# Eleven pieces of the gate's projection move from the first unit of pairs into the quads

## Chip, core and metric

One NeuronCore of a Trainium2 chip runs the whole program in one launch. The metric is the device time of an execution in microseconds; lower is better. Engines are called by short names: PE (TensorE, matmuls and transposes), DVE (VectorE), ACT (ScalarE), POOL (GpSimd) and SP (SyncE, which here issues all the DMAs).

## What is computed

Two layers of a hybrid encoder over 768 tokens (a sequence of 256 and one of 512), width 2048, in fp32:

```python
h = rms_norm(x, ln_g[l])
qa, ka, va, ga, qb, kb, vb, gb, qc, kc, vc, gc = split(h @ w_in[l])
ya = window_sink_attention(...)        # mixer A: +-128 tokens, a sink, relative bias
yb = global_axial_attention(...)       # mixer B: dense, rotary
yc = dilated_mixture_attention(...)    # mixer C: (window, dilation) (128,1), (512,4), (2048,16), merged
mix = concat([ya * silu(ga), yb * silu(gb), yc * silu(gc)])
x = x + mix @ w_out[l]
```

The 32 heads have 64 columns each; mixers A and B have 12 query heads, C has 8 for each of three dilations. The gate is the product of h with 2048 columns of w_in.

## The kernel before, in words

Each layer has three stages. First the projection of all columns but the gate's, in nine slabs of 512 columns. Last the output product. Between them lies the attention, and the gate's projection is dealt out in pieces over it; this stage is what the change touches.

**Precision.** Each fp32 operand of a large product is split in two parts, hi (a rounded copy, made by ACT) and lo (the rest, made by DVE); a product is three matmuls, hi·hi, hi·lo and lo·hi.

**Steps.** The attention is a list of 216 steps, written out in Python before the program is built. Steps 0 to 23 are the quads (kind Q: the dilated parts of mixer C, four heads at a time, one token tile per item). They come in four units of six: steps 0 to 5 and 12 to 17 are open (dilation 4), 6 to 11 and 18 to 23 are packed (dilation 16, four classes in one tile). Steps 24 to 47 are the first unit of pairs (mixer A, two heads of an item, one head per step), then come the other pairs of A, C and B up to step 215.

**Turns.** All engines walk through one loop over turns i (232 of them per layer, N_LOOP), in a fixed order of instructions. In turn i PE does the scores of step i, then the gate's pieces of this turn, then the product with v of an earlier pair (PAIR_LAG 5), the transpose of the probabilities of step i-3 (T_LAG) and, for quads and C, the product with v of step i-4 (V_LAG). DVE adds the bias and takes the minimum of the scores of step i (find_minima), ACT takes the exponential (exp_step), DVE takes its reciprocal and POOL normalises one turn later in the pairs (NORM_LAG). DVE or ACT takes the quads' results out of their bank in turn i+5 (take_part for open, take_packed for packed items), and SP stores them (store_part). There are two banks for scores, so the scores of step i wait for the minima of step i-2.

**The gate.** There are 16 gate tiles of 128 columns; each takes 16 chunks of k times two halves of the tokens, so 512 pieces in a layer. A piece is three matmuls of 128 x 384. 16 pieces are done ahead of the loop, 20 behind step 215, and the 476 between them are dealt over the steps by piece_schedule, in proportion to a cost per step. PIECES_BY[i] is how many pieces are done by the end of turn i. Much else is timed from it by turn_of_piece:

- SPLIT_TURN: when ACT (split_hi, w_hi) and DVE (split_lo, w_lo) split a chunk of 128 x 512 gate weights. In the quads DVE does this behind the minima of the turn, ACT behind the exponentials.
- GATE_LOADS_AT: behind which item SP issues the next 512 KB of gate weights (two chunks; w_raw has three slots).
- DRAIN_TURN, TANH_AT, SILU_TURN, PRODUCT_TURN: when DVE takes a finished gate tile half out of its bank, ACT makes the tanh, POOL the silu and the product with the attention's result.

**SP's order.** For each item `it` from 4 on, SP waits for the scores of item it-4, loads the queries of item it (quad_t in the quads, 256 KB), stores parts of quads that are due, then loads keys, values, the blocks of the packed units (the values, laid out by class), the bias and last the gate weights that stand at this item. The blocks of unit 3 (steps 18 to 23) are loaded in four parts, at items 20 to 23; the product of step 18, in turn 22, needs all of them.

```python
for it in range(Q_SLOTS, N_ITEMS + 1):
    load_item(l, it)
    for i in PARTS_AT.get(it, ()): store_part(l, i)
    ...
    for u, c in BLOCKS_AT.get(it, ()): load_blocks(l, u, c)
    for b, heads in BIASES_AT.get(it, ()): load_bias(l, b, heads)
    ...
    for m in GATE_LOADS_AT.get(it, ()): load_weights(l, CHUNKS_IN // PER_LOAD + m)
```

Of the kernel before, what the change touches and what calls it, by code (L numbers as in the profile page):

```python
# [310 lines left out]
def packed(unit):  # L311

    return unit["kind"] == "Q" and unit["g"] == 2
# [6 lines left out]
def attention_items():  # L320

    order = [x for u in range(len(ATT_UNITS)) for x in unit_items(u)]
    items, steps = [], []
    for u, hp, t in order:
        unit = ATT_UNITS[u]
        lo, hi = next(x for x in SEQ_TILES if x[0] <= t < x[1])
        a, b = max(lo, t - unit["reach"]), min(hi, t + unit["reach"] + 1)
        for r in (None,) if hp is None else (0, 1):  # L330
            first = min(max(t * P - C_REACH, lo * P), hi * P - C_KEYS) if unit["kind"] == "C" else a * P
            tiles = (1 if packed(unit) else 4) if r is None else C_KEYS // P if unit["kind"] == "C" else b - a
            steps.append(dict(item=len(items), u=u, unit=unit, kind=unit["kind"], hp=hp, t=t, r=r, a=a, first=first,
                              tiles=tiles, last=r != 0))
        items.append(dict(u=u, unit=unit, kind=unit["kind"], hp=hp, t=t, step=len(steps) - 1))
    return items, steps


ITEMS, STEPS = attention_items()
# [225 lines left out]

def piece_schedule():

    cost = [3 if packed(st["unit"]) else {"Q": 1}.get(st["kind"], 8) for st in STEPS]
    done, now, between = [], 0, PIECES - PIECES_FIRST - PIECES_LAST
    for i in range(N_LOOP):  # L570
        if i < N_STEPS:
            now += cost[i]
            done.append(PIECES_FIRST + between * now // sum(cost))
        else:
            done.append(min(PIECES, PIECES - PIECES_LAST + PIECES_LAST * (i - N_STEPS + 1) // V_LAG))
    assert done[-1] == PIECES
    return done


PIECES_BY = piece_schedule()  # L580


# [2102 lines left out]
```

How the kernel before makes its waits and increments, by code:

```python
        def prob_copied(eng, l, i):  # L926
            if features_first(STEPS[i]) or not on_act(i):
                eng.wait_ge(pt_dve, l * DVE_COPIES[-1] + DVE_COPIES[i])
            else:
                eng.wait_ge(pt_act, l * ACT_COPIES[-1] + ACT_COPIES[i])
# [1 line left out]
        def turn_evacuated(eng, i):  # L933
            l, s, t, b, _ = TURNS[i]
            if s == "norm":
                eng.wait_ge(norm_lo, NORM_AT[l, s, t, b] + 1)
            else:
                eng.wait_ge(turned_lo, HEAD_AT[l, s, t] + 1)
# [17 lines left out]
        def quad_taken(eng, l, quad):  # L957
            item = QUADS[quad]
            if packed(item["unit"]):
                eng.wait_ge(packed_taken, l * N_PACKED + item["packed_no"] + 1)
            else:
                eng.wait_ge(part_taken, l * (N_QUADS - N_PACKED) + item["open_no"] + 1)
# [1 line left out]
        def bias_in(eng, l, b):  # L965
            sets = [x for x in BIAS_SETS if BIAS_NO[x] % 2 == b % 2]
            each_layer = sum(4 if x[1] is None else 2 for x in sets)
            in_layer = sum(4 if x[1] is None else 2 for x in sets if BIAS_NO[x] <= b)
            eng.wait_ge(bias_loaded[b % 2], 16 * (l * each_layer + in_layer))
# [5 lines left out]
        def stat_free(eng, pair):  # L976
# [3 lines left out]
            l, at = divmod(pair - STAT_SLOTS, N_PAIRS)  # L980
            old = PAIRS[at]
            if old["kind"] == "C":
                eng.wait_ge(merge_chain, 5 * (l * MERGES + old["merge_no"] // TT) + 5)
            else:
                eng.wait_ge(normed, l * NORMED[-1] + NORMED[old["step"]])
```

## Time and profile before

| | |
|---|---|
| Median of three executions | 2765.29 us (2764.78 to 2768.25) |
| The profiled execution | 2772.11 us, span 2769.8 us |
| Granted PE clock over the span | 0.994 of full speed |
| Busy: PE matmuls / PE weight loads / DVE / ACT / POOL | 99% / 88% / 58% / 43% / 28% |
| DMA | 442.52 MB, 160 GB/s |
| Quads, layer 0 / layer 1 | 651.0 to 706.3 / 2021.8 to 2082.7 us |

The span runs from the first to the last instruction. A matmul's busy time overlaps its neighbours' (they are pipelined, and their ends are modelled), so what a series of matmuls costs is read from start to start, and not from their durations. The granted clock of a stretch is the mean over it; PE has two levels, 2.4 GHz (1.00) and 1.2 GHz (0.50).

### The profile page before, as it was taken

The numbers are of one execution on the slowest core, as the hardware profiler recorded it, in microseconds if no ns is written. First come the engines' busy times: TensorE is split into PE (matmuls) and PEld (weight loads), VectorE is DVE, ScalarE is ACT, GpSimd is POOL, SyncE is SP. The second block draws the span as 40 slices with busy tenths as digits, with TensorE's granted clock in tenths as the row PEclk, the third lists the DMA queues.
The fourth block names the chain that finished last, engine by engine and source line by source line (L and its number), as shares of the span: only waits on it lengthen the run. The fifth ranks groups of instructions, "written<-read, shape, count | busy, mean of one in ns | idle before, by whom it ended". The sixth has DMA issues, their size and how long they took to land. (4 is left out here: it accounts for less than half of the span.)

```text
span 2769.8 us, 43315 instructions
## 1 busy us (share of the span) xinstructions
PE 2732.1 (99%) x14505; PEld 2447.6 (88%) x14505; DVE 1609.7 (58%) x3865; ACT 1184.4 (43%) x2813; POOL 763.8 (28%) x882
## 2 busy tenths in 40 slices
PE   8999999999999999999999999999999999999999
PEld 7888899988999999988888888999889999999887
DVE  3345644434676677677743465444346767776776
ACT  4322222224565566544542222222246655665443
POOL 0333333320343344300003334333203433443000
PEclk9999999999999999999999999999999999999999
DMA  5356566668544542464524565656774445325535
GB/s 175 106 183 200 180 185 188 181 179 233 142 132 123 128 112 82 177 219 130 197 85 142 176 195 173 200 170 188 191 218 134 117 118 149 101 69 217 192 122 182
DMA packets 436214, 442.52 MB, mean 160 GB/s; under 512 B 97591, under 2 KB 327127, under 8 KB 435996
## 3 DMA queue, kind: packets, MB, share of 16 engines
q1 hardware_dynamic: 435996, 439.77, 53.3%
q8 instruction: 118, 1.93, 0.3%
q14 instruction: 100, 0.82, 0.1%
HBM read 313.91 MB, written 125.75 MB: 159 GB/s over the span
## 5 line engine op out<-in xcount | busy, mean ns | idle before, releaser
L1834 ACT CAST w_hi<-w_raw 128x512 fp32r<-128x512 f32 x640 | 397.0, 622 | 697.8 <-PE bank L1605 430.6
L1603 PE MATMUL bank<-w_hi,act_hi 128*128 128x512 f32 x1728 | 689.2, 399 | 0.0
L2120 DVE TENSOR_TENSOR w_lo<-w_raw,w_hi 128x512 fp32r<-128x512 f32 x640 | 460.1, 722 | 384.9 <-ACT w_hi L1834 383.3
L1605 PE MATMUL bank<-w_hi,act_lo 128*128 128x512 f32 x1728 | 679.0, 393 | 0.0
L1604 PE MATMUL bank<-w_lo,act_hi 128*128 128x512 f32 x1728 | 677.6, 392 | 0.0
L1605 PEld LDWEIGHTS bank<-w_hi,act_lo 128*128 128x128 f32 x1728 | 372.6, 216 | 54.1
L1603 PEld LDWEIGHTS bank<-w_hi,act_hi 128*128 128x128 f32 x1728 | 373.3, 216 | 50.1
L1604 PEld LDWEIGHTS bank<-w_lo,act_hi 128*128 128x128 f32 x1728 | 373.3, 216 | 48.7
L1659 PE MATMUL bank<-act_hi,w_hi 128*128 128x384 f32 x1024 | 349.2, 341 | 0.0
L1661 PE MATMUL bank<-act_hi,w_lo 128*128 128x384 f32 x1024 | 346.3, 338 | 0.0
L1660 PE MATMUL bank<-act_lo,w_hi 128*128 128x384 f32 x1024 | 345.7, 338 | 0.0
L2561 POOL TENSOR_SCALAR prob<-prob,denom 128x256 f32<-128x256 f32 (+2 forms) x288 | 165.6, 577 | 399.1 <-DVE denom L2275 398.8
L1636 PE MATMUL bank<-w_hi,a_part 128*128 128x512 f32 x672 | 263.0, 391 | 2.7 <-DVE x_cols L2416 2.0
L1637 PE MATMUL bank<-w_lo,a_part 128*128 128x512 f32 x672 | 261.6, 389 | 0.0
L1638 PE MATMUL bank<-w_hi,a_part 128*128 128x512 f32 x672 | 261.5, 389 | 0.0
L2266 DVE TENSOR_TENSOR pt_lo<-bank,pt_hi 128x256 fp32r<-128x256 f32 (+2 forms) x288 | 154.0, 535 | 184.8 <-ACT pt_hi L1934 182.3
L2552 POOL TENSOR_TENSOR y<-y,gains 128x256 f32<-128x256 f32 (+1 forms) x144 | 159.9, 1123 | 265.5 <-DVE y L2153 265.5
L2186 DVE TENSOR_TENSOR turned<-bank,turned 128x512 fp32r<-128x512 f32 (+2 forms) x120 | 64.8, 556 | 277.4 <-ACT turned L1901 277.4
L1901 ACT CAST turned<-bank 128x512 fp32r<-128x512 f32 (+2 forms) x120 | 55.2, 481 | 364.2 <-PE bank L1581 355.8
L1660 PEld LDWEIGHTS bank<-act_lo,w_hi 128*128 128x128 f32 x1024 | 194.1, 190 | 4.2
L1709 PE MATMUL bank<-ident,prob 128*128 128x128 f32 x1128 | 195.7, 274 | 1.5 <-POOL prob L2561 0.9
L1659 PEld LDWEIGHTS bank<-act_hi,w_hi 128*128 128x128 f32 x1024 | 193.5, 189 | 4.1
(136 smaller groups left out, 4406.5 us busy)
## 6 DMA issues: line engine op xcount, KB each, us to landing
w_raw<-w_in SPq DMA_DIRECT2D x144, 512.0 KB, 4.8
w_sums<-sum_out SPq DMA_DIRECT2D x32, 1280.0 KB, 6.7
w_raw<-w_sums SPq DMA_DIRECT2D x80, 512.0 KB, 4.0
sum_in<-w_out SPq DMA_DIRECT2D x64, 512.0 KB, 5.6
heads_t<-turned SPq DMA_DIRECT2D x240, 128.0 KB, 2.4
q_t<-heads_t SPq DMA_DIRECT2D x192, 128.0 KB, 2.1
k_t<-keys_t SPq DMA_DIRECT2D x48, 384.0 KB, 5.8
w_raw<-w_out SPq DMA_DIRECT2D x32, 512.0 KB, 3.7
```

The source lines that it names most:

```text
L1603: pe.matmul(acc[t][:], hi, w_hi[:, W_AT[n]:W_AT[n] + SLAB], start=(k == 0), stop=False)
L1604: pe.matmul(acc[t][:], hi, w_lo[:, W_AT[n]:W_AT[n] + SLAB], start=False, stop=False)
L1605: last = pe.matmul(acc[t][:], lo, w_hi[:, W_AT[n]:W_AT[n] + SLAB], start=False, stop=(k == KC - 1))
L1636: pe.matmul(bank[at][:], hi[:, tokens], w_hi[:, W_AT[n]:W_AT[n] + SLAB], start=(j == 0), stop=False)
L1637: pe.matmul(bank[at][:], hi[:, tokens], w_lo[:, W_AT[n]:W_AT[n] + SLAB], start=False, stop=False)
L1638: last = pe.matmul(bank[at][:], lo[:, tokens], w_hi[:, W_AT[n]:W_AT[n] + SLAB], start=False, stop=(j == KH - 1))
L1659: pe.matmul(out, hi, act_hi[:, k, tokens], start=(k == 0), stop=False)
L1660: pe.matmul(out, hi, act_lo[:, k, tokens], start=False, stop=False)
L1661: last = pe.matmul(out, lo, act_hi[:, k, tokens], start=False, stop=(k == KC - 1))
L1709: last = pe.transpose(pt_bank[n % PT_BANKS][:, j * P:(j + 1) * P], prob[:, n % P_SLOTS, j * P:(j + 1) * P], ident[:])
L1834: nc.scalar.copy(w_hi[:, W_AT[n]:W_AT[n] + SLAB], w_raw[:, load % W_RAW, j, :]).then_inc(w_hi_done, 1)
L2120: nc.vector.tensor_tensor(w_lo[:, W_AT[n]:W_AT[n] + SLAB], w_raw[:, load % W_RAW, j, :], w_hi[:, W_AT[n]:W_AT[n] + SLAB].bitcast(F32), ALU ...
```

## The change

```diff
 def piece_schedule():
 
-    cost = [3 if packed(st["unit"]) else {"Q": 1}.get(st["kind"], 8) for st in STEPS]
+    first_pairs = min(st["u"] for st in STEPS if st["kind"] != "Q")
+    cost = [4 if packed(st["unit"]) else 3 if st["kind"] == "Q" else 6 if st["u"] == first_pairs else 8 for st in STEPS]
     done, now, between = [], 0, PIECES - PIECES_FIRST - PIECES_LAST
     for i in range(N_LOOP):
         if i < N_STEPS:
```

The cost of a packed quad's step goes from 3 to 4, that of an open quad's from 1 to 3, that of a step of the first unit of pairs from 8 to 6; all others stay at 8. Since the pieces are dealt in proportion, PIECES_BY changes, and with it the tables that are timed from it:

| | before | after |
|---|---|---|
| pieces in the quads' turns 0 to 23 | 14 | 25 |
| pieces in turns 24 to 47 | 58 | 44 |
| pieces in turns 48 to 215 | 404 | 407 |
| turns with one piece among 0 to 23 | 3, 6 to 11, 14, 17, 19 to 23 | 1 to 7, 9 to 20, 22, 23 (two in 8 and 21) |
| splits of gate chunks 4 to 11 in turns | 9, 15, 22, 25, 33, 35, 37, 38 | 5, 9, 12, 16, 30, 33, 35, 37 |
| third and fourth gate load in the loop, at item | 20, 29 | 14, 21 |
| tile 0's second half taken out, tile 1's first, in turns | 25, 32 | 16, 28 |

From gate tile 2 on the tables differ by at most two turns.

## Rows read from the trace of the kernel before

**Rows 1.** The page, busy time and share of each engine.

```profile
PE 2732.1 (99%) x14505; PEld 2447.6 (88%) x14505; DVE 1609.7 (58%) x3865; ACT 1184.4 (43%) x2813; POOL 763.8 (28%) x882
```

**Rows 2.** Busy time by stretch: us, PE, PEld, DVE, ACT, POOL, clock, DMA share, GB/s.

```profile
651.00:706.30 55.30, 48.03 (x358) 45.58 (x356) 35.26 (x166) 26.74 (x85) 1.99 (x2) 0.91 0.86 246
706.30:757.00 50.70, 50.70 (x332) 49.92 (x331) 32.71 (x141) 31.84 (x95) 20.17 (x31) 1.00 0.45 125
2021.80:2082.70 60.90, 52.98 (x357) 50.25 (x356) 34.86 (x166) 26.79 (x85) 2.01 (x2) 0.85 0.81 223
2082.70:2135.00 52.30, 52.30 (x336) 51.41 (x335) 33.07 (x142) 32.27 (x96) 20.55 (x31) 0.97 0.45 122
```

**Rows 3.** PE's timeline in the quads: start, us, instruction, idle before and its releaser.

```profile
659.52 0.33 PE L1689 MATMUL bank<-k_t,quad_t 128*128 128x128 f32 x1 [1.23 <-DMA quad_t<-heads_t]
...
678.46 0.30 PE L1689 MATMUL bank<-k_t,quad_t 128*128 128x128 f32 x1 [1.46 <-DVE part_out L2237]
...
702.76 1.21 PE L1731 MATMUL bank<-blocks,prob_t 128*128 128x260 f32 x2 [4.35 <-DMA blocks<-v_rows]
...
2032.63 0.63 PE L1684 MATMUL bank<-k_t,quad_t 128*128 128x64 f32 x4 [1.38 <-DMA quad_t<-heads_t]
...
2053.88 0.30 PE L1689 MATMUL bank<-k_t,quad_t 128*128 128x128 f32 x1 [1.26 <-DVE part_out L2237]
...
2079.14 1.21 PE L1731 MATMUL bank<-blocks,prob_t 128*128 128x260 f32 x2 [4.97 <-DMA blocks<-v_rows]
```

**Rows 4.** Busy time by finer stretches of the quads, columns as in rows 2.

```profile
659.52:673.93 14.41, 14.41 (x113) 13.83 (x114) 10.58 (x37) 5.03 (x16) 0.00 (x0) 1.00 0.86 238
673.93:683.68 9.75, 8.29 (x51) 7.54 (x51) 4.34 (x33) 6.10 (x23) 0.00 (x0) 0.82 1.07 301
683.68:702.76 19.08, 14.73 (x123) 14.28 (x122) 11.78 (x49) 7.79 (x23) 0.00 (x0) 0.92 0.93 269
702.76:706.29 3.53, 3.52 (x12) 3.14 (x13) 2.48 (x8) 1.35 (x4) 0.00 (x0) 0.50 0.18 58
...
2030.50:2049.56 19.06, 17.68 (x101) 16.91 (x100) 10.22 (x33) 4.80 (x15) 0.00 (x0) 0.73 0.76 198
2049.56:2059.10 9.54, 8.28 (x51) 7.53 (x51) 4.14 (x33) 6.10 (x23) 0.00 (x0) 0.82 0.92 243
```

**Rows 5.** PE's timeline: two gate pieces' starts, and scores in the first pairs.

```profile
643.24 0.34 PE L1659 MATMUL bank<-act_hi,w_hi 128*128 128x384 f32 x1
...
643.76 0.34 PE L1659 MATMUL bank<-act_hi,w_hi 128*128 128x384 f32 x1
...
722.21 0.42 PE L1695 MATMUL bank<-k_t,q_t 128*128 128x384 f32 x1
```

**Rows 6.** Timelines of DVE and ACT in layer 0's quads.

```profile
677.20 0.29 DVE L2237 CUSTOM_DVE_ANT_0 prob<-bank,bias 128x128 f32<-128x128 f32 x1 [2.14 <-DMA bias<-bias_rows]
...
684.14 1.28 ACT L1916 ACTIVATE prob<-prob,part_out 128x128 f32<-128x128 f32 x4 [1.05 <-DVE part_out L2237]
685.33 0.60 ACT L1834 CAST w_hi<-w_raw 128x512 fp32r<-128x512 f32 x1
...
685.96 0.69 DVE L2120 TENSOR_TENSOR w_lo<-w_raw,w_hi 128x512 fp32r<-128x512 f32 x1 [1.25 <-ACT w_hi L1834]
...
702.38 0.29 DVE L2200 TENSOR_TENSOR prob<-bank,bias 128x128 f32<-128x128 f32 x1 [4.64 <-DMA part_rows<-part_out]
```

**Rows 7.** SP's timeline of DMA issues in layer 0's quads.

```profile
673.00 0.43 SPq L1302 DMA_DIRECT2D bias<-bias_rows  x1
...
686.22 0.32 SPq L1381 DMA_DIRECT2D part_classes<-part_out  x1
...
696.59 0.89 SPq L1278 DMA_DIRECT2D blocks<-v_rows  x2
```

**Rows 8.** Waits of PE's weight loads from 706 to 760, and POOL's timeline there.

```profile
PEld bank L1709 <- POOL prob L2561: 0.4, 1, 0.4
...
724.67 0.58 POOL L2561 TENSOR_SCALAR prob<-prob,denom 128x384 f32<-128x384 f32 x1 [1.67 <-DVE denom L2275]
```

## The prediction

> **What bounds the kernel now.** I read the page first: its busy line says that TensorE (PE) is busy 2732.1 of 2769.8 us, the next engine, VectorE (DVE), 58% [rows 1]. A change that neither adds nor drops a matmul can therefore only win where PE is not busy, or where it is busy at the lower clock. So the second view is busy time by stretches, one for the quads (items of kind Q, steps 0 to 23) and one for the first unit of pairs (steps 24 to 47), in each layer [rows 2]. The reader is to see two different regimes. In the quads PE has 48.03 of 55.3 us and 52.98 of 60.9 us, the granted clock is 0.91 and 0.85, and the DMA engines are at 0.86 and 0.81. In the first pairs PE is busy for all of the 50.7 and 52.3 us, the clock is 1.00 and 0.97, DVE has 65% and GpSimd (POOL) 40%. Time moved from the second into the first can be hidden; time in the second is paid in full.
>
> Third, PE's own timeline in the quads: which wait ends last [rows 3]. Three waits of over 1 us stand in each layer; counting the groups of scores in front of them gives their steps. Layer 0: 1.23 us before the scores of step 5 (its quad_t load), 1.46 us before those of step 14 (DVE's minima of step 12, themselves late), 4.35 us before the product of step 18, in turn 22 (the blocks load); 7.04 us in all. Layer 1: 1.38 (quad_t of step 6), 1.26 (step 14), 4.97 us (blocks); 7.61 us.
>
> Fourth, the clock in finer stretches [rows 4]. A stretch of w us at granted clock c spent 2(1-c)w us at the lower of the two levels, 1.2 GHz, and the matmuls in it lost half of that, (1-c)w. That gives in layer 0 1.75 us (673.93 to 683.68) and 1.77 us (702.76 to 706.29), and in layer 1 5.15 and 1.72 us, and 1.6 us at the head of the first pairs [rows 2, 4]. Each fall of the clock comes behind one of the waits. Not each wait brings one: behind the 1.23 us wait of layer 0 the clock stands at 1.00 (659.52 to 673.93), the 1.38 us wait of layer 1 is followed by the dearest one. Check: layer 1's quads are 5.6 us longer than layer 0's; waits (0.57) and half speed (5.1) account for 5.7.
>
> **The change, part by part.** It alters only the list of shares from which piece_schedule deals the gate's 476 middle pieces. Recomputing that list by hand for both: up to step 23 each layer has 14 pieces before and 25 after; steps 24 to 47 have 58 before and 44 after; the 3 left over are spread over the later steps. No matmul is added or dropped.
>
> *A piece* is three matmuls. From one start of line 1659 to the next is 0.52 us [rows 5]. The Trainium skill has another figure ("TensorE: Matmul & The Clock Gate", Back-to-back issue gap: in a real stream about 131 ns per matmul of 512 columns, less for narrower ones), by which a piece were at most an estimated 0.39 us and the sum below some 1.5 us smaller. The row here is 174 ns at 384 columns, and the trace decides.
>
> *Out of the first pairs:* 14 x 0.52 = 7.3 us, to be had in full, as PE there is never idle. *Into later steps:* 3 x 0.52 = 1.6 us, paid in full: PE is as busy there. Net 5.7 us off, per layer.
>
> *Into the quads:* 11 x 0.52 = 5.7 us per layer, less what the waits take up. I go by the wait.
>
> First wait: scores of step 1 release the load of step 5's quad, and between them PE now has one piece more in each of turns 1, 2 and 4: 1.6 us against 1.23. Layer 1: turns 2, 4 and 5, 1.6 against 1.38. Both gone, and with the second goes the half speed behind it, 5.15 us.
>
> Second wait: DVE's minima of step 12 start 2.14 us late for the bias load [rows 6] that SP issues at 673.00 [rows 7] once the scores of step 10 are done. Two pieces more in turns 12 and 13, 1.0 us: 0.4 and 0.2 us are left. Here the moved splits bite. SPLIT_TURN moves with the pieces: gate chunks 4, 5, 6, 7 are split in turns 9, 15, 22, 25 before and 5, 9, 12, 16 after, one split more in the quads. In such a turn DVE's minima are followed by w_lo, which waits for ScalarE's (ACT) exp and w_hi; behind it are queued the minima of the next step, and for those waits PE with the scores two steps on. With turn 12 holding a split: exp 1.28, w_hi 0.60, w_lo 0.69 [rows 6], four minima at 0.29 less overlap, about 0.9: 3.5 us from the minima of step 12 to those of step 13, where PE has one turn of about 1.3 us (44 us of full-speed work over 24 steps is 1.8 with today's pieces) plus its added piece: 1.8 to 1.9. A new wait of about 1.6 us before step 15, in both layers. Its bounds: nothing, if ACT takes the split beside the exp, and 3.5. The half speed behind step 14 I leave as it is. At turns 5, 9 and 16 the quads' packed steps or the second s_bank cover the same 3.5 us.
>
> Third wait: the blocks. SP issues without a pause from part 11 (686.22) to the last pair of blocks (696.59) [rows 7], with 512 KB of gate weights in between, and that last pair lands 5.3 us after its issue ends at 697.48, when the wait does (702.76) [rows 3]. The load at item 20 goes to item 14, but the next one comes from item 29 to item 21, still ahead of the last two blocks: same number of issues, same bytes at nearly the same place. The train starts when ACT has taken quad 11; from there to the wait PE gets 3 pieces more (turns 16, 18, 21): 1.5 us off, leaving 2.8 and 3.4. Bounds: nothing off, or worse by 512 KB at 269 GB/s, 1.9 us, as the DMA engines are at 0.93 there [rows 4]; and 5.7 us off if the train starts earlier. The store of part 14, for which DVE waits 4.64 us in turn 22 [rows 6], lands in the same moment and moves with the blocks. Half speed behind it stays.
>
> *Sum on the profiled execution.* Layer 0: waits 7.04 to 4.8 (0.4, 1.6, 2.8), so +5.7 - 2.2 - 5.7 = -2.2. Layer 1: waits 7.61 to 5.2, half speed -5.15, so +5.7 - 2.4 - 5.15 - 5.7 = -7.5. Together -9.7 on its own 2772.1 us. That execution is 6.8 us above the median of the three runs, 2765.3. The 5.15 us stretch may be part of that excess: layer 0 shows that nearly the same wait can pass without it. Without it the gain is 4.6. I take the middle, 7.2: 2758 us.
>
> **Rivals.** *More comes back (0.28).* With PE denser, the wait before step 15 doesn't come (1.6 x 2) and the half speed behind step 14 goes (1.75 + 1.72): 6.7 more, 2751.5 us. For it: every fall of the clock stands behind a wait. Against it: ACT and DVE are strictly in order.
>
> *The last wait doesn't shrink (0.14).* SP's train is released by PE's progress; if it starts later by what PE was given, waits stay 4.35 and 4.97: 3.0 us of the gain go, 2761; with the 1.9 us for bytes in each layer up to 2765. For it: DMA at 0.93. Against: 1.5 us of added work lie behind the train's release.
>
> *The first pairs aren't bound by PE any more (0.08), the case on the other side.* Their step falls from 50.7/24 = 2.11 us to 1.81, and the transpose of a step, three turns on, waits for DVE's minimum, ACT's exp, DVE's reciprocal and POOL's normalise. From the scores (722.21) to the end of the normalise (725.25) that is 3.0 us [rows 5, 8]; a gate's silu, two POOL operations of about 1 us, can stand ahead: 5.1 against 5.4. Today 0.4 us is lost that way in 54 [rows 8]. If the step doesn't get shorter at all, 2 x 7.3 us of the gain are gone: 2772.7. It decides from a step of about 2.07 us on (12.7 us lost over 48 steps), which would be 3.0 us of chain stretched to 6.2, so I hold it for unlikely.
>
> *No effect to be seen (0.05):* waits come back wherever pieces leave, 2765.
>
> **How the numbers follow.** What this kernel's timing can tell from no change is about 0.2%, 5.5 us. My forecast has 0.45, of which 0.38 lies below 2759.8. Faster: 0.38 + 0.28 = 0.66. Within: 0.07 + 0.14 + 0.03 = 0.24. Slower: 0.08 + 0.02 = 0.10. The likeliest case alone is 2754 to 2761; for 8 in 10 I take 2749.5 to 2764, which holds the first three cases to their bounds.
>
> **What would show it.** Right: PE without a wait before steps 5 and 6, and layer 1's clock at 1.00 from 2030 on; a new wait before step 15 with w_lo in turn 12; blocks waits near 3 us; first pairs 43 to 44 us long with PE busy throughout. Wrong: quads longer by all of 5.7 us, a transpose of the first pairs waiting on POOL, or the clock's falls elsewhere than behind the waits named.

## The result and the profile after

The changed kernel takes 2774.49 us (median of 7 runs, 2773.04 to 2779.92), the kernel before 2765.29 beside it. The ratio is 1.0035, with a 95% interval of 1.0024 to 1.0047: the change makes the kernel 9.2 us slower. I had forecast 2758. The profiled execution took 2779.92 us, the slowest of its seven.

Up to the first scores of layer 0 the changed kernel's profile is 1.4 us shorter (649.61 us against 651.04); elsewhere outside the attention the two differ by 0.1 us. Inside the attention I cut both at the starts of the scores. A stretch of steps is the time from the start of the scores of its first step to that of the step behind it.

| steps | layer 0 before, after | layer 1 before, after | change predicted per layer |
|---|---|---|---|
| 0 to 23, quads | 55.25, 62.50 | 60.88, 59.39 | +3.5 and -1.8 |
| 24 to 47, first pairs | 49.41, 49.04 | 50.59, 47.66 | -7.3 |
| 48 to 71 | 51.28, 53.60 | 51.30, 53.59 | +0.5 (58 pieces, 57 before) |
| 72 to 214 | 331.6, 332.9 | 331.7, 332.4 | +1.0 (two more pieces) |

The first pairs lost 14 of 58 pieces and are hardly shorter, and the unit behind them, which got one piece more, is 2.3 us longer. Busy time of the changed kernel by the same stretches, columns as in [rows 2]:

```profile
649.61:712.11 62.50, 55.90 (x390) 52.23 (x389) 36.86 (x168) 28.25 (x88) 4.04 (x4) 0.91 0.80 226
712.11:761.15 49.04, 47.07 (x282) 41.76 (x281) 30.76 (x134) 29.07 (x89) 17.66 (x28) 0.97 0.42 119
761.15:814.75 53.60, 51.95 (x334) 49.07 (x335) 39.03 (x158) 35.28 (x101) 25.42 (x37) 1.00 0.40 113
2031.02:2090.41 59.39, 54.01 (x389) 50.77 (x389) 36.43 (x167) 27.83 (x87) 4.03 (x4) 0.94 0.85 235
2090.41:2138.07 47.66, 45.76 (x282) 40.53 (x281) 31.26 (x136) 29.29 (x89) 17.65 (x28) 1.00 0.45 126
```

The reader is to compare the second and the third column of the first pairs. PE's busy time fell from 49.41 to 47.07 us, that of its weight loads from 48.63 to 41.76. The first of before is in the row below, the same stretch cut at the scores:

```profile
706.29:755.70 49.41, 49.41 (x325) 48.63 (x323) 31.89 (x137) 30.57 (x93) 19.83 (x30) 1.00 0.46 129
```

So there is idle time now, nearly 7 us of it by the weight loads, and it is made up of many short waits. Waits of PE's weight loads in the first pairs of the changed kernel (in us: total, times, longest):

```profile
PEld bank L1710 <- issue: 2.4, 5, 0.6
PEld bank L1696 <- issue: 2.1, 7, 0.4
PEld bank L1766 <- DVE pt_lo L2267: 1.2, 5, 0.3
PEld bank L1710 <- POOL prob L2562: 0.7, 1, 0.7
```

**What sets the pace there** is DVE's own timeline. In the kernel before, DVE in two steps of the first pairs:

```profile
733.52 0.48 DVE L2257 CUSTOM_DVE_ANT_0 prob<-bank,bias,sinks 128x256 f32<-128x256 f32 x1
...
735.04 0.56 DVE L2266 TENSOR_TENSOR pt_lo<-bank,pt_hi 128x384 fp32r<-128x384 f32 x1 [1.03 <-ACT pt_hi L1934]
...
735.63 0.48 DVE L2257 CUSTOM_DVE_ANT_0 prob<-bank,bias,sinks 128x256 f32<-128x256 f32 x1
```

And in the changed kernel, DVE, then ACT:

```profile
738.99 0.48 DVE L2258 CUSTOM_DVE_ANT_0 prob<-bank,bias,sinks 128x256 f32<-128x256 f32 x1
...
740.50 0.56 DVE L2267 TENSOR_TENSOR pt_lo<-bank,pt_hi 128x384 fp32r<-128x384 f32 x1 [1.03 <-ACT pt_hi L1935]
...
741.10 0.48 DVE L2258 CUSTOM_DVE_ANT_0 prob<-bank,bias,sinks 128x256 f32<-128x256 f32 x1
...
743.70 0.48 DVE L2258 CUSTOM_DVE_ANT_0 prob<-bank,bias,sinks 128x256 f32<-128x256 f32 x1
```

```profile
739.50 0.51 ACT L1929 ACTIVATE prob<-prob,minus_max 128x257 f32<-128x257 f32 x1 [1.16 <-DVE minus_max L2258]
...
740.02 0.45 ACT L1935 CAST pt_hi<-bank 128x384 fp32r<-128x384 f32 x1
```

This is a ring, the same in both kernels. The minima of step i (738.99) release ACT's exp of step i (739.50). Behind it in ACT's queue stands the upper copy of the turned probabilities of step i-3 (740.02), though PE had finished the transposes that it copies some 2 us earlier (738.04). It releases DVE's lower copy (740.50, after 1.03 us of waiting), and behind that in DVE's queue stand the minima of step i+1 (741.10). This round takes 2.11 us. The next one has a w_lo, a fold addition and a gate drain as well and takes 2.60.

PE is no member of the ring. The test of that is DVE's own pace, from the minima of step 28, where the ring has set in, to those of step 47, 19 rounds later (before, then changed):

```profile
716.36 0.48 DVE L2257 CUSTOM_DVE_ANT_0 prob<-bank,bias,sinks 128x256 f32<-128x256 f32 x1
...
756.77 0.48 DVE L2257 CUSTOM_DVE_ANT_0 prob<-bank,bias,sinks 128x256 f32<-128x256 f32 x1
```

```profile
721.87 0.48 DVE L2258 CUSTOM_DVE_ANT_0 prob<-bank,bias,sinks 128x256 f32<-128x256 f32 x1
...
762.63 0.48 DVE L2258 CUSTOM_DVE_ANT_0 prob<-bank,bias,sinks 128x256 f32<-128x256 f32 x1
```

That is 40.41 us before and 40.76 after (in layer 1 40.41 and 40.69), although PE has 45 pieces in these turns before and 35 after. A round takes 2.13 us on average.

In the kernel before, PE's work happened to take almost as long, 2.06 us a step. The two banks for scores let PE run ahead of DVE by up to two steps, and that slack hid the slower ring: the minima of step 24 start 0.8 us behind their scores, those of step 47 3.2 us. PE looked busy without a gap, and was.

In the quads, the waits of PE that answer to those of [rows 3], PE's timeline of the changed kernel:

```profile
678.81 0.30 PE L1690 MATMUL bank<-k_t,quad_t 128*128 128x128 f32 x1 [1.45 <-DVE part_out L2238]
680.97 1.24 PE L1732 MATMUL bank<-blocks,prob_t 128*128 128x260 f32 x2 [0.39 <-ACT prob_t L1163]
...
708.58 1.20 PE L1732 MATMUL bank<-blocks,prob_t 128*128 128x260 f32 x2 [4.46 <-DMA blocks<-v_rows]
...
2060.70 0.30 PE L1690 MATMUL bank<-k_t,quad_t 128*128 128x128 f32 x1 [1.81 <-DVE part_out L2238]
...
2088.57 0.68 PE L1732 MATMUL bank<-blocks,prob_t 128*128 128x260 f32 x2 [2.55 <-DMA blocks<-v_rows]
```

The waits before steps 5 and 6 are gone, as forecast. That before step 14 did not shrink (it even grew in layer 1, from 1.26 to 1.81 us), though two pieces were put ahead of it, and the one for the blocks shrank in layer 1 alone. DVE's and SP's timelines say why for step 14:

```profile
677.55 0.29 DVE L2238 CUSTOM_DVE_ANT_0 prob<-bank,bias 128x128 f32<-128x128 f32 x1 [3.34 <-DMA bias<-bias_rows]
...
680.52 0.69 DVE L2121 TENSOR_TENSOR w_lo<-w_raw,w_hi 128x512 fp32r<-128x512 f32 x1 [1.85 <-ACT w_hi L1835]
...
691.54 0.69 DVE L2121 TENSOR_TENSOR w_lo<-w_raw,w_hi 128x512 fp32r<-128x512 f32 x1 [2.38 <-ACT w_hi L1835]
```

```profile
672.26 0.43 SPq L1303 DMA_DIRECT2D bias<-bias_rows  x1
672.74 0.49 SPq L1198 DMA_DIRECT2D w_raw<-w_in  x1
```

The bias is waited for 3.34 us where it was 2.14 [rows 6]. The moved gate load is now issued right behind it. The two splits in the third unit of quads make DVE wait 1.85 and 2.38 us.

What these splits cost PE shows only in part as a wait above (0.39 us at 680.97). A matmul's recorded end is modelled, so the cost is read from start to start. Scores of steps 14 and 15 of the changed kernel, then of the kernel of experiment 4, which has the same pieces but no split in turns 12 and 16:

```profile
678.81 0.30 PE L1690 MATMUL bank<-k_t,quad_t 128*128 128x128 f32 x1 [1.45 <-DVE part_out L2238]
...
682.20 0.45 PE L1690 MATMUL bank<-k_t,quad_t 128*128 128x128 f32 x1
```

```profile
676.30 0.41 PE L1691 MATMUL bank<-k_t,quad_t 128*128 128x128 f32 x1
...
678.28 0.41 PE L1691 MATMUL bank<-k_t,quad_t 128*128 128x128 f32 x1
```

Step 14 takes 3.39 us with the split in turn 12 (3.39 in 15 of the 16 layers of the eight runs that have it, 3.52 in the other), and 1.97 to 1.99 in the six layers of experiments 3, 4 and 7 that don't: 1.4 us per layer. Step 18 takes 2.8 us or more with the split in turn 16 and 2.3 in the six, another 0.5 us.

### The profile page after: what moved, and what is told of

It is laid out like the page before. It is cut to its first block and busy times, and to the rows that moved or that the text cites. A ratio compares the mean times of both kernels' runs of the same rounds, so it can differ in the third digit from the quotient of the medians.

```text
span 2777.6 us, 43315 instructions
## 1 busy us (share of the span) xinstructions
PE 2736.8 (99%) x14505; PEld 2442.0 (88%) x14505; DVE 1613.8 (58%) x3865; ACT 1186.4 (43%) x2813; POOL 765.0 (28%) x882
## 5 line engine op out<-in xcount | busy, mean ns | idle before, releaser
L1606 PEld LDWEIGHTS bank<-w_hi,act_lo 128*128 128x128 f32 x1728 | 372.5, 216 | 53.8
L1902 ACT CAST turned<-bank 128x512 fp32r<-128x512 f32 (+2 forms) x120 | 55.3, 482 | 364.5 <-PE bank L1582 355.6
```

What stands on the lines that cost most here:

```text
L1606: last = pe.matmul(acc[t][:], lo, w_hi[:, W_AT[n]:W_AT[n] + SLAB], start=False, stop=(k == KC - 1))
```

## The experiments

Times are medians; each ratio, with its 95% interval, is to runs of the kernel before on the same chip (whose median was 2763.5 to 2765.1). It is not the quotient of the two medians and differs from it by up to 0.001, some 3 us. "Changed" means the changed kernel. Times of stretches and steps are from single executions.

**1. Is PE the bound of the pairs?** Two runs take pieces out of the kernel before and put them nowhere.

```
+LEFT_OUT = [33, 37, 38, 45, 49, 50, 57, 61, 69, 73, 81, 85]
...
-                        gate_piece(l, p)
+                        if p not in LEFT_OUT:
+                            gate_piece(l, p)
```

> The kernel before, with 12 of the 58 gate pieces in turns 24 to 47 of each layer (the steps of the first unit of pairs) left out of the computation and put nowhere else; their splits and drains stay in their turns. So the gate misses 12 of its 512 pieces. The prediction's own theory, that TensorE sets the pace of the first pairs: 12 x 0.52 us x 2 layers = 12.5 us faster, about 2752.8. The ring theory: in the first pairs the pace is set by the row minima on VectorE, exp and the upper copy of the turned probabilities on ScalarE, and the lower copy on VectorE, one after the other in each step; TensorE only gains a slack of some 3 us. So 0 to 2 us faster, about 2764, and the scores of the turns from 24 to 48 take 48 to 49.5 us in each layer as before (49.41 and 50.59).

Measured 2761.38 us, ratio 0.9994 (0.9985 to 1.0003), not to be told from before's and far from the 12.5 us on offer. First pairs: 48.38 and 48.71 us. The weight loads' busy time there is 42.34 us against 48.63, 6.3 us less, which is what 12 pieces of 0.52 us are. The stretch got 1.0 and 1.9 us shorter, not 6.2, and DVE's minima of steps 28 to 47 lie 40.43 and 40.40 us apart, as before.

> The control to the run before it: the kernel before, with 14 gate pieces in turns 144 to 176 of each layer (steps of unit 9 on, behind the C units) left out and put nowhere else. If TensorE sets the pace there: 14 x 0.52 x 2 = 14.6 us faster, about 2750.7. If VectorE and ScalarE set it there too: 0 to 2 us faster. The steps there take 2.4 us each with 115.9 us for turns 144 to 192, against 2.1 in the first pairs; I lean to 8 to 14 us faster.

Measured 2760.20 us, ratio 0.9985 (0.9976 to 0.9995): a gain of some 4 us where 14.6 were on offer. My lean to 8 to 14 us was wrong. In these B units too, PE's time is mostly not what a step costs; the C units (steps 96 to 143) were not tried.

**2. Break the ring.** In the pairs the upper copy goes ahead of the exp, so that the copy, whose data is ready, no longer stands behind an exp that waits for DVE.

```
-                    if not quads and i < N_STEPS:
-                        exp_step(l, i)
                     if 0 <= i - T_LAG < N_STEPS:
                         pt_copy(l, i - T_LAG)
-                    if quads:
+                    if i < N_STEPS:
                         exp_step(l, i)
```

> The kernel before with one order changed: in the steps of the pairs ScalarE does the upper copy of turn i-3 ahead of the exp of step i, not behind it. Ring theory: the lower copy on VectorE, and with it the next row minima, no longer wait for the exp of the same step (0.6 to 0.8 us of a wait of 1.04 us in each step). In this kernel TensorE has hardly an idle time in the first pairs, so little is gained there: 0 to 4 us faster over both layers. If instead the exp comes too late for the transposes three turns on, it is slower. The theory that TensorE sets the pace alone: no difference.

> The changed kernel with the same order changed (in the pairs the upper copy of turn i-3 ahead of the exp of step i). Ring theory: the 11 pieces taken out of the first pairs are now worth their time, so turns 24 to 48 of each layer take 42 to 45 us (49.04 and 47.66 in the changed kernel), and the time falls by 8 to 14 us against the changed kernel, to 2760 to 2766. If TensorE's own work, not the ring, sets the pace, it stays at 2774 (within 2 us).

The kernel before with this order: 2754.59 us, ratio 0.9966 (0.9954 to 0.9979), 10 us less, more than expected; its steps 48 to 71 go from 51.3 to 49.4 us. Changed with this order: 2758.41, ratio 0.9979 (0.9970 to 0.9988), 16 us below the changed kernel (the 11 pieces of the expectation are the 14 taken out). Its first pairs take 43.36 and 42.68 us, against 49.65 and 50.17 in the other: 6.3 and 7.5 us for 14 pieces out, close to the 7.3 of the prediction. DVE's minima of steps 28 to 47 are 33.96 and 34.08 us apart instead of 40.7. Busy time by stretch (first pairs, then steps 48 to 71) and DVE's timeline of changed with this order:

```profile
711.49:754.85 43.36, 43.23 (x282) 41.90 (x281) 32.88 (x138) 30.15 (x92) 17.72 (x29) 0.98 0.47 132
754.85:804.72 49.87, 49.87 (x338) 49.47 (x336) 41.30 (x159) 33.66 (x98) 25.31 (x37) 1.00 0.45 126
```

```profile
735.53 0.47 DVE L2256 CUSTOM_DVE_ANT_0 prob<-bank,bias,sinks 128x256 f32<-128x256 f32 x1
...
736.16 0.56 DVE L2265 TENSOR_TENSOR pt_lo<-bank,pt_hi 128x384 fp32r<-128x384 f32 x1 [0.15 <-ACT pt_hi L1935]
...
736.84 0.48 DVE L2256 CUSTOM_DVE_ANT_0 prob<-bank,bias,sinks 128x256 f32<-128x256 f32 x1
```

The wait for the upper copy is 0.15 instead of 1.03 us, and two minima can be 1.31 us apart. DVE and ACT have the same work as in the changed kernel, so it was their order, the ring, that kept the first pairs long. The order also ends most of the +2.3 us of steps 48 to 71: they take 49.87 us against 49.38 in before with this order, and 0.5 us is the one piece more.

**3. What the 11 pieces cost the quads by themselves.** The kernel before, with repeats of a piece in the turns that the change fills:

```
                     for p in range(first, end):
                         gate_piece(l, p)
+                    for _ in range(EXTRA.count(i)):
+                        extra_piece(l, i)
```

> The kernel before, whole, with 11 more pieces of the same three matmuls in each layer, in the turns of the quads in which the change does one more; they repeat work of the gate (into its bank, with no wait and no signal of their own), and every piece, split, load and drain of before stays in its turn. If the pieces themselves cost the quads what the prediction summed (5.7 us each layer less 2.2 taken up by waits in layer 0): 3 to 4 us per layer, 2771 to 2773. If the pieces are taken up by the waits for the bias and the blocks and the rest of the changed kernel's cost comes from the splits and loads that moved with them: 0 to 2 us per layer, 2764 to 2768. I lean to the second, as the changed kernel with its splits and loads moved took 52.8 and 53.1 us in the quads of the two layers.

Measured 2766.30 us, ratio 1.0010 (1.0001 to 1.0020): 22 pieces, 11.4 us of matmuls, cost 2.8 us. The waits of the quads do take up most of the pieces. Without the new wait behind the split, the prediction's terms for them come to 1.9 and 1.7 us, 3.6 together, so this part was about right (the 3 to 4 us per layer of the expectation had the split's wait in them). The rest of what makes the changed quads long is what moved along.

**4. The splits.**

```
+SPLIT_TURN.update({4: 7, 5: 10, 6: 19, 7: 22})
 SPLIT_AT = at_turns(SPLIT_TURN.items())
```

> The changed kernel with the splits of chunks 4 to 7 of each layer, which the change had put into turns 5, 9, 12 and 16, done in turns 7, 10, 19 and 22, so none of them in the third unit of quads, where ScalarE has four exps of 0.3 us in each step. All pieces stay where the change put them. In the changed kernel turns 14 to 18 take 13.8 us (10.3 before) with three pieces more (1.6 us). If the rest is the wait of the lower split for the upper one and what is queued behind it (1.85 and 2.38 us waits of VectorE at turns 12 and 16, new PE waits at steps 15 and 16, and the stretch at half speed behind them), turns 14 to 18 go to 11.8 to 12.3 us and the time falls by 3 to 6 us over both layers, to 2768 to 2771. If the added pieces themselves bring it out, by pushing the transposes back, it stays within 1 us of 2774.5.

Measured 2763.80 us, ratio 0.9994 (0.9982 to 1.0006): 10.7 us below the changed kernel, level with before, and about twice what I expected. This edit isn't pure: the items of the gate loads are worked out from the split turns, so they went from 14 and 21 to 15 and 27. No run moves the splits alone. The nearest to it is the comparison with the first run of experiment 5, on the same chip, where both loads are out of the way but the splits stay: 2767.91, so 4.1 us are left for the splits, and the 1.4 and 0.5 us of steps 14 and 18 make 3.9 over both layers. The profiled execution (the fastest of its twelve, 2759.32) has the quads at 52.81 and 53.06 us, with the clock at 1.00:

```profile
648.77:701.58 52.81, 50.64 (x390) 48.30 (x389) 35.27 (x164) 27.59 (x87) 4.01 (x4) 1.00 0.89 254
```

```profile
699.73 0.68 PE L1733 MATMUL bank<-blocks,prob_t 128*128 128x260 f32 x2 [1.33 <-DMA blocks<-v_rows]
```

**5. The loads.** Each run changes one line behind the table of loads, here the first:

```
+GATE_LOADS_AT[20], GATE_LOADS_AT[29] = GATE_LOADS_AT.pop(14), GATE_LOADS_AT.pop(21)
```

> The changed kernel with its two gate loads that moved forward on SP (items 14 and 21) put back to items 20 and 29, all else as changed. If the load of 786 KB beside the bias transfer is what makes the bias land 1.2 us later at step 14, that wait falls from 3.3 to about 2.1 us and the time by 1 to 3 us over both layers; if the bias wait is set by its issue and its queue alone, the time stays within 1 us. I lean to no difference, as turns 12 to 14 grew by 1.1 us and two pieces account for 1.04.

Measured 2767.91 us, ratio 1.0014 (1.0005 to 1.0023), 6.6 us below changed. I leaned the wrong way. (A gate load is 512 KB, not 786.)

> The changed kernel with the first of its two moved gate loads put back alone (item 14 to 20; the second stays at item 21). The first load is issued right behind the transfer of the first part of the bias for the third unit of quads, and the second in front of block loads of the fourth. With both back the time was 2767.9, 6.6 us less. If the first is what counts (bias wait at step 14 and the half-speed stretch behind it, 1.1 and 2 us in each layer): 2768 to 2770, with turns 22 to 24 still at 5.5 to 9 us. If the second one counts: 2773 to 2775.

> The counterpart: the changed kernel with the second moved gate load alone put back (item 21 to 29). If the first load counts: 2772 to 2775. If the second one counts, since it lies among the four block loads for the fourth unit of quads (blocks wait of 4.46 us in layer 0 and 2.5 in layer 1): turns 22 to 24 fall to about 4.7 us in each layer and the time by 2 to 5 us, to 2770 to 2772.

Measured 2776.34 (ratio 1.0046, 1.0031 to 1.0061) and 2775.48 (1.0047, 1.0032 to 1.0062): neither gains alone. Three more runs (the last on the kernel before: `GATE_LOADS_AT[24] = GATE_LOADS_AT.pop(20)`):

> The changed kernel as it is, run beside the two below, since the single loads put back measured 2776.3 and 2775.5, both together 2767.9, on other chips than the changed kernel's own 2774.5. The sum of the single effects by stretch (2.0 and 1.3 us per layer) against both together (6.1 per layer) can only be read if the changed kernel stands where it stood: ratio to before 1.003 to 1.0045, time 2773 to 2776. If instead it is at 1.006 or more here, the single loads had an effect that the different chips hid.

> The changed kernel with its first moved load at item 16 (it has 14; behind all four parts of the bias for the third unit, which go at 11 to 14, and ahead of the next at 17) and the second at item 24 (it has 21; behind the last of the four block loads, at 20 to 23). So both lie nearer to the changed kernel's places than to before's 20 and 29, but clear of the bias and block loads. If it is their place among these loads that costs: 2766 to 2769, as with both back at 20 and 29 (2767.9). If it is that they come early at all, by whatever they share the DMA engines with: 2771 to 2775.

> The kernel before with one edit: its own gate load at item 20, issued between the first two block loads for the fourth unit of quads, goes to item 24, behind the last. If the load among the block loads is what makes PE wait 4.35 and 4.97 us for the blocks: turns 22 to 24 fall from 9.2 and 9.8 us (7.0 to 8.5 in the other kernels with before's places) to 5 to 6 us and the time by 4 to 7 us, to 2757 to 2760. If the blocks wait for something else (their own issue by SP behind the waits of the stores, or the bias transfer): within 1.5 us of 2764.

Changed again: 2774.96 (1.0046, 1.0029 to 1.0063), where it stood. Loads at 16 and 24: 2773.38 (1.0033, 1.0021 to 1.0045). By stretch of the profiled executions, in us, both layers added:

| kernel | loads at items | steps 12 to 15 | 18 to 21 | 22, 23 | sum | median |
|---|---|---|---|---|---|---|
| changed again | 14, 21 | 23.3 | 20.7 | 13.3 | 57.3 | 2774.96 |
| first back | 20, 21 | 20.4 | 20.2 | 19.1 | 59.7 | 2776.34 |
| second back | 14, 29 | 26.1 | 19.9 | 11.7 | 57.6 | 2775.48 |
| clear of both | 16, 24 | 20.0 | 26.2 | 7.6 | 53.8 | 2773.38 |
| both back | 20, 29 | 19.8 | 19.9 | 9.4 | 49.1 | 2767.91 |
| splits moved | 15, 27 | 18.6 | 19.7 | 8.5 | 46.7 | 2763.80 |

A load at 14 lengthens steps 12 to 15 (bias), two loads at 20 and 21, side by side, lengthen 22 and 23 (blocks), and a load at 16 lengthens 18 to 21. Putting one back moves the cost from one column to another. Only both clear, or the splits out of the way too, takes it off. So it is neither place alone nor earliness alone. The executions of "both back" and "splits moved" are the fastest of theirs, 5.4 and 4.5 us under the median, so their sums flatter them somewhat.

The load at 16 has its own victim. DVE's minima of step 16 wait for the store of an earlier part (part_classes) to land, 2.8 and 2.6 us in the two layers where they wait 1.1 and 0.9 with both loads back, and PE then waits 1.9 and 1.7 us for a copy of DVE in step 18, which is 1.6 and 1.4 us longer. In layer 1 the lower clock follows: steps 19 and 20 take 3.2 us more, the latter wholly at 1.2 GHz. That is the 6.3 us by which steps 18 to 21 are longer over both layers. That the store lands late because of the load is argued from its place alone.

The kernel before with its own load behind the blocks: 2760.87, ratio 0.9991 (0.9980 to 1.0003). Steps 22 and 23 take 7.2 and 7.8 us, where the three kernels of experiments 1 and 2 that have before's places and pieces take 7.9 to 9.3. That is some 1 us a layer; the expected 5 to 6 us did not come, and the time can't be told from before's: this load is not the main thing that makes the blocks late there. What is, no run shows.

The half speed goes with these waits. Busy time of the changed kernel from 682 to 690 us (steps 15 and 16), and of "both back" over its quads of layer 0:

```profile
682.00:690.00 8.00, 8.00 (x43) 7.51 (x42) 3.46 (x27) 5.47 (x18) 0.00 (x0) 0.64 0.78 203
```

```profile
648.46:702.38 53.92, 50.91 (x389) 48.15 (x389) 36.40 (x167) 27.75 (x87) 4.02 (x4) 1.00 0.86 249
```

At 0.64, 2 x 0.36 x 8.0 = 5.8 us of these 8 were at 1.2 GHz, and up to 2.9 us lost; from start to start steps 15 and 16 are 2.6 us longer than in "both back". Ahead of it PE had waited 1.45 us (678.81) and 0.39 (680.97). With "both back" these waits are 0.33 and 0.40, and the clock stays at 1.00.

**6. Turns in which split, fold and drain meet.**

```
+for c in range(LEAD + 1, CHUNKS_GATE + LEAD):
+    if 48 <= SPLIT_TURN[c] < 96:
+        SPLIT_TURN[c] = max(SPLIT_TURN[c] + SPLIT_TURN[c] % 2, SPLIT_TURN[c - 1] + 1 + (SPLIT_TURN[c - 1] + 1) % 2)
```

> The changed kernel with the splits of turns 48 to 95 in even turns alone (48, 50, 52, 54, 62, 64, 66, 68, 74 and so on, in place of 48, 50, 51, 53, 61, 63, 65, 66, 74). The additions of the folded pairs on VectorE lie in odd turns. If the 2.3 us by which turns 48 to 72 are longer in each layer than before come from turns in which split, fold and gate drain meet on VectorE (51, 53, 61, 63, 65, 66), this stretch goes from 53.6 to 51.3 us and the time falls by 4 to 5 us. If they come from the slack having been used up ahead of turn 48 and not from where the splits lie, no difference.

One gate load moves along with them, from item 49 to 50.

Measured 2772.06 us, ratio 1.0031 (1.0021 to 1.0041), 2.4 us below changed, with intervals that overlap; steps 48 to 71 take 52.96 us, 0.6 less, not 2.3. The theory explains a quarter of PE's time. It does better on DVE's own: its minima of steps 48 to 71 span 49.12 us before, 50.43 in the changed kernel and 49.46 here, so the splits make 1.0 of DVE's 1.3 us. The other half of the 2.3 us is at step 70, which takes 3.21 us against 2.16 before, and is untouched by this edit. PE's weight loads and POOL there, in the changed kernel:

```profile
812.31 0.31 PEld L1710 LDWEIGHTS bank<-ident,prob 128*128 128x128 f32 x3 [1.05 <-POOL prob L2562]
```

```profile
810.67 1.02 POOL L2584 TENSOR_TENSOR mixed_t<-mixed_t,gate_t 128x384 f32<-128x384 f32 x1
811.68 0.58 POOL L2562 TENSOR_SCALAR prob<-prob,denom 128x384 f32<-128x384 f32 x1
```

DVE's reciprocal was done at 810.74, but POOL's normalise stood behind a product of 1.02 us. In changed with the order of experiment 2 the view of waits lists none for PE's weight loads in the whole unit. The other theory, that the slack was used up ahead of turn 48, doesn't hold: the minima of step 48 start 3.64 us behind their scores before and 3.74 after.

**7. All together.** Experiments 2, 4 and 6 in one kernel:

> The changed kernel with three edits together: ScalarE's upper copy ahead of the exp in the pairs, the splits of chunks 4 to 7 in turns 7, 10, 19 and 22, and the splits of turns 48 to 95 in even turns. With the first alone it measured 2758.4. If the costs add: 3 to 6 us less from the quads and 0 to 2 from the even turns (the stretch 48 to 72 is 49.9 us there already), so 2751 to 2755, at or below the kernel before with the order changed alone (2754.6). If the moved work costs its own time in the quads, it stays at 2757 to 2759.

Measured 2746.84 us (6 runs), ratio 0.9944 (0.9926 to 0.9962): 17 us below before and 28 below the changed kernel, and better than expected. Against the kernel before with the order alone (2754.6, on another chip) the moved pieces, with their splits put right, are now worth some 6 us by the ratios and 8 by the medians. That is near the 7.2 us of the forecast, which is partly luck: 2.6 us of those stood for a stretch at half speed that no run bears out. Steps 48 to 71 take 49.87 us, the same as without the third edit, which adds nothing there. Its quads and first pairs of layer 0:

```profile
650.95:704.56 53.61, 51.51 (x390) 48.87 (x389) 36.05 (x165) 27.95 (x87) 4.03 (x4) 0.99 0.89 252
704.56:748.33 43.77, 43.55 (x283) 41.97 (x281) 33.69 (x142) 30.32 (x92) 17.79 (x29) 0.98 0.52 144
```

## Why the prediction was wrong

**The step that failed** is "14 x 0.52 = 7.3 us, to be had in full, as PE there is never idle". The price of a piece was right (12 pieces out took 6.3 us from the weight loads' busy time). That the time could be had was not: a second limit of almost the same size, the ring of ACT and DVE at 2.13 us a step on average, lay beside PE's own 2.06. The stretch shortened by 0.4 and 2.9 us in the profiled executions. That is 11.3 us less gain over both layers than forecast.

**The rival on the other side** had the right symptom, first pairs that don't get shorter, and its time (2772.7) is 2 us from the result. That nearness is luck: its criterion, a step of about 2.07 us or more, was just missed (2.04 and 1.99 us), and the rest of the slowdown came from the quads and steps 48 to 71. It named the wrong chain and got 0.08. I followed one step's data from its scores to POOL's normalise, 3.0 us against three turns, and found slack. A chain along the data of one step has a latency. What set the pace was a cycle through the order of two queues, with data of steps i and i-3, and a cycle has a period, which no slack hides. POOL did hold PE for 1.05 us once a layer, at step 70, and once for 0.7 us in layer 0's first pairs.

**Later steps, "paid in full".** Steps 72 to 214 are 1.4 and 0.7 us longer for two more pieces, near their 1.0. But steps 48 to 71, where one piece more stood for 0.5 us, cost 2.3 us a layer: 1.3 us in DVE's turns, most of it from the moved splits, and 1.05 us at step 70, where POOL's normalise came behind a product. I had followed the splits in the quads alone.

**Quads, first wait.** Right: the waits before steps 5 and 6 are gone.

**Quads, second wait.** The new cost of the split in turn 12 came, and at its size: w_lo waits 1.85 us, and step 14 is 1.4 us longer where I had 1.6. The split in turn 16, which I had held to be covered, costs 0.5 us at step 18; those in turns 5 and 9 were covered (steps 5 to 11 take 15.3 us, as in experiment 3, which leaves them where they were). The wait before step 14, which was to shrink to 0.4 and 0.2, stayed at 1.45 and grew to 1.81, because the moved load lies behind the bias: with both loads back it is 0.33 in layer 0. I had said "the load at item 20 goes to item 14" and weighed it for the blocks only.

**Quads, third wait.** 4.46 and 2.55 us against 2.8 and 3.4: my upper bound in one layer, under my value in the other.

**Half speed, -5.15 in layer 1.** The stretch belonged to the one profiled execution. In the four other kernels whose quads are as before (one with its load at 24), which ran without it, steps 5 to 11 of layer 1 take 14.5 us, not 20.7. I had seen that doubt and kept half of the term; it should have been none. The check that seemed to bear it out had left out other half speed: by [rows 2] the two layers' quads differ in it by 0.15 x 60.9 - 0.09 x 55.3 = 4.1 us, not 5.1. Against the four kernels' quads, on average 53.3 us in layer 0 and 55.1 in layer 1, the changed ones' (60.2 to 62.5, and 56.2 to 59.4) are some 5.2 us a layer longer, where without this term I had 3.5 and 3.3.

Together, starting from the 4.6 us gain without the half-speed term: 11.3 less from the first pairs, 3.6 from steps 48 to 71 and about 3.6 from the quads make 14 us slower. The measured 9.2 (6.6 to 13.0 by the interval) is less; the terms come from single executions, and those of the changed kernel spread over 7 us.

## What to carry to other kernels

An engine that is busy without a gap proves that it is *a* limit, not that it is the only one. Before costing work taken from it at full price, find the pace that the others would keep without it: take two starts of the same instruction one step apart on each of the other engines, follow who waited for whom between them, and if the path closes through two in-order queues, its period is a floor. A wait that comes back in most steps on an engine with 60% load (here DVE for ACT, 16 times in the stretch, 11.8 us in all, five of them of 1.03 or 1.04 us) marks such a ring, and what cured it here was the queue order that lets ready work go ahead of work that waits.

When a schedule is dealt from a list of shares, everything that is worked out from it moves too. Here the pieces cost 2.8 us, the loads that went with them 6.6 and the splits about 4, each known to 3 or 4 us only.

## What was not expected of the hardware

PE's busy time hides a wait that its weight loads show. With 12 pieces left out (experiment 1), 6.2 us of work, PE's busy time in the first pairs of layer 0 fell from 49.41 to 47.25 us, that of the weight loads from 48.63 to 42.34. A PE column at 96 to 98% can therefore stand for 10% of room; the column of weight loads is the one to read.

The fall of the clock to 1.2 GHz behind a wait can't be told from the wait's length alone. When the changed kernel ran again, steps 14 and 15 of its two layers, which hold the same work, read (busy time by stretch):

```profile
677.45:685.00 7.55, 7.05 (x32) 5.85 (x32) 3.57 (x26) 6.38 (x22) 0.00 (x0) 0.65 1.07 274
2055.19:2060.76 5.57, 4.66 (x31) 3.91 (x32) 3.36 (x26) 4.40 (x16) 0.00 (x0) 1.00 1.07 264
```

The first came behind a wait of 0.77 us and was mostly at the lower level; the second came behind 1.10 us and kept 2.4 GHz. The 1.98 us between them are all in step 15. It is not mere chance either. In the five runs that have the load at item 14 and the split in turn 12 (the changed kernel twice, with the order of experiment 2, with the second load back, with the splits of experiment 6), step 15 takes 3.8 or 4.2 us in 8 of 10 layers and 2.18 in two; in the three runs with that split but the load at 16 or 20 it takes 2.18 in all six, behind shorter waits (step 13, which holds the wait, takes 2.3 to 2.8 us there, 3.1 to 4.2 in the five). So the schedule sets how likely such a fall is, and a forecast can carry its price only as a chance.
